# A hybrid decoder step on one core: where the decode attention gets its first operands, who splits its last values, and how the dense phase begins

## The chip, the cores and the metric

The kernel runs on one core of a Trainium2 chip. A time is the device time of one execution in microseconds (us). Three runs of the kernel before gave 1883.61, 1886.72 and 1889.7 us, so the median is 1886.72 us. The profile is one further execution of 1886.89 us.

## The reference, cut to what matters

One layer serves a prompt of 512 tokens and a sample group of 8 sequences with 8 new tokens each (64 rows). All arithmetic is float32.

```python
xn = rmsnorm(x, norm1_g);  proj = xn @ w_in          # q, k, v of 4 head sets, forget gates, 2 branch gates
q, k = rmsnorm per head (and rope in the 3 dilated sets)
# sample group, per sequence b: one paged set (FoX) and three windows
k_past = cache_fox_k[0][page_table]                   # 32 pages of 128 rows, 8 heads x 64
s = q @ k_past^T * scale + cnew + suffix(logf);  p = softmax(s with the 8 new keys);  o = p @ v_past + p_new @ v_new
# the same over window rows of cache_win1..3_kv, the three merged by their log-sum-exp
# prompt group: causal FoX attention and banded dilated attention
mixed = sigmoid(gate_a) * (o_fox @ w_branch_a) + sigmoid(gate_b) * (o_dil @ w_branch_b)
h = x + mixed @ w_out;  u = relu(rmsnorm(h) @ w_up);  y = h + (u * u) @ w_down
```

The outputs are y of both groups, the new k and v rows, the forget values and the shifted window caches.

## The kernel before, in words

Four functions run one after the other, with a barrier of all engines between them: `project_tokens` (0 to 488 us of the profile), `attend_sample` (488 to 1133), `attend_prompt` (1133 to 1341) and `finish` (1341 to the end). To keep float32 accuracy in the fast matmul form, each operand is split into a high part (a rounded copy, `*_hi`) and a low part (the difference, `*_lo`), and two or three products are summed.

`attend_sample` walks through 8 sequences (batches) of 24 groups each: 16 FoX groups of two pages, then 8 window groups of one or two tiles of 128 rows. A tile of K or V is 256 KB. Each engine has its own instruction stream, written out by `straight` (line 801): at step n an engine does each of its stages for group n minus the stage's delay. The stages of group i are:

- SP, step i: loads K of group i (`load_keys`) once group i - 6 is turned (a ring of 6 slots), with a load of the bias row for each even FoX group; step i + 20: loads V of group i (`load_values`), also in a ring of 6, freed when the low part of V of group i - 6 is made.
- PE, step i: turns K (transposes into `ktp`, line 1253); step i + 2: scores (line 1269); step i + 21: turns the probabilities; step i + 22: sums the values into `o_ps` (line 1285).
- ACT, step i: `kt_hi` (line 1082); step i + 20: exponentials and `vv_hi` (lines 1069 and 1090).
- DVE, step i + 1: `kt_lo` (line 1108); step i + 3: bias and maximum; step i + 21: the splits of the probabilities; in the last batch also `vv_lo` of two groups in three (line 1166).
- POOL, step i + 20: `vv_lo` (line 1024).

The `vv` buffers are a ring of 3, so `vv_hi` of group i waits for the sum of group i - 3.

Before its first K load, SP issues the page table and eight loads of the new queries and keys (lines 922 to 925), which lie as 64 columns inside the scratch tensors `qt_s` and `kt_s`. ACT and DVE split all of them first (lines 1052 and 1103) and POOL lays all queries out (line 998). At SP's step 2 come five small loads (lines 961 and 962): forget values, a triangle, two masks, and the new values `vs_raw`. A small matmul at PE's step 1 (line 1257) sums the new forget values in a bank of `s_ps`, and the first scores wait for its result. The new values are split by ACT at step 6 (line 1075) and POOL at step 8 (line 1007), both into buffers of the `vv` ring; SP stores them to scratch at step 14 in six stores (line 968). `qn_raw`, `kn_raw` and `vs_raw` lie in slots 0 to 3 of the V ring, which is why V loads come later.

`finish` begins with one weight slab (two halves: branch a, branch b) split by ACT (line 1862) and DVE (line 1929), then the attention output `o_all` split in two pieces of four tiles (lines 1867 and 1933); PE starts when the slab and the first piece are there (line 2016).

Of the kernel before, what the change touches and what calls it, by code (L numbers as in the profile page):

```python
# [13 lines left out]
P = 128  # L14
D_MODEL = 1024
SEQ = 512
# [42 lines left out]
def project_tokens(nc, a, sem, ident):  # L59

    with ExitStack() as ctx:
# [116 lines left out]
        def _(sp):  # L178
# [31 lines left out]
            sp.dma_start(cum[:], a["c_cum"]).then_inc(cum_in, 16)  # L210

# [26 lines left out]
            for s in range(SETS):  # L238
                g = s - 1
                for c in range(3):  # L240
# [532 lines left out]

def late_values(b, i):

    return isinstance(b, int) and b == DEC_BATCH - 1 and i >= PER_BATCH - EXP_BEHIND and i % 3 != 0
# [43 lines left out]
def attend_sample(nc, a, sem, ident, o_t, qk_raw, pair_in):  # L820

    with ExitStack() as ctx:
# [7 lines left out]
        pages = sb("pages", [1, DEC_BATCH * N_PAGES], I32)  # L830
# [45 lines left out]
        pages_in, in_small, queries_in, sample_v_in = sem("p2_pages_in"), sem("p2_small_in"), sem("p2_queries_in"), sem("p2_sample_v_in")  # L876
# [15 lines left out]
        held, v_lo_late = sem("held"), sem("v_lo_late")  # L892
# [9 lines left out]
        def values_split(eng, b, i):  # L902

            late = sum(late_values(b, n) for n in range(i + 1))
            if late_values(b, i):
                eng.wait_ge(v_lo_late, late)
            else:
                done(eng, v_lo, group_index(b, i) - late)
# [12 lines left out]
        def _(sp):  # L921
            sp.dma_start(pages[:], a["page_table"].rearrange("b n -> (b n)").unsqueeze(0)).then_inc(pages_in, 16)
            for s in range(SETS):
                sp.dma_start(qn_raw[:, s], a["qt_s"][s, :, :, SEQ:N_TOK].rearrange("q p n -> p q n")).then_inc(queries_in, 16)
                sp.dma_start(kn_raw[:, s], a["kt_s"][s, :, :, SEQ:N_TOK].rearrange("q p n -> p q n")).then_inc(queries_in, 16)
# [23 lines left out]
            def load_keys(b, i):  # L949
                done(sp, k_turned, group_index(b, i) - RAW_RING)  # L950
                hold(sp)
                load("K", a["cache_fox_k"], k_raw, k_in, b, i)
                if group_kind(i) == FOX and i % 2 == 0:
# [5 lines left out]
                if isinstance(b, int) and b == 0 and i == 2:  # L959
# [3 lines left out]
                if isinstance(b, int) and b == 0 and i == 14:  # L963
# [20 lines left out]
        def _(gp):  # L984
# [33 lines left out]
            def values_lo(b, i):  # L1018
                slot, tiles = i % VV_RING, group_tiles(i)
                if isinstance(b, int) and b == 0 and i == 0:  # L1020
                    gp.wait_ge(vs_stored, 96)
                if not late_values(b, i):
                    done(gp, v_hi, group_index(b, i))
                    gp.tensor_tensor(vv_lo[:, slot, 0:tiles, :], v_raw[:, i % RAW_RING, 0:tiles, :], vv_hi[:, slot, 0:tiles, :].bitcast(F32),  # L1024
                                     ALU.subtract).then_inc(v_lo, 1)
                if i == 7:
# [3 lines left out]
                    for part, x in enumerate((vn_hi, vn_lo)):  # L1030
# [16 lines left out]
        def _(act):  # L1047
            for s in (k_hi, v_hi, p_done):
                act.sem_inc(s, PER_BATCH)
            act.wait_ge(queries_in, 16 * 2 * SETS)  # L1050
            for dst, src in ((qn_hi, qn_raw), (kn_hi, kn_raw)):
                act.activation(dst[:], src, ACT.Copy).then_inc(parts_hi, 1)

            act.wait_ge(parts_lo, 2)
# [17 lines left out]
            def keys_hi(b, i):  # L1072
                if isinstance(b, int) and b == 0 and i == 6:
# [10 lines left out]
            def values_hi(b, i):  # L1084
# [1127 lines left out]
```

## Time and profile before

| | before |
|---|---|
| median of three runs | 1886.72 us (1883.61 to 1889.7) |
| profiled execution | 1886.89 us |
| its span, first to last instruction | 1885.1 us |
| PE / weight loads busy | 1739.2 / 1543.9 us (92% / 82%) |
| DVE, ACT, POOL busy | 1094.9, 956.1, 871.2 us |
| granted TensorE clock, mean | 0.97 |
| q1 (all loads and stores of SP) | 422.63 MB |

The execution is 1.8 us longer than its span; that part lies outside the program's instructions. The page divides the span into 40 slices of 47.1 us. In those from 500 to 1080 us PE and the DMA engines are both at nine tenths or more; in the dense phase after 1341 us only PE is.

### The profile page before, as it was taken

The numbers are of one execution on the slowest core, as the hardware profiler recorded it, in microseconds if no ns is written. First come the engines' busy times: TensorE is split into PE (matmuls) and PEld (weight loads), VectorE is DVE, ScalarE is ACT, GpSimd is POOL, SyncE is SP. The second block draws the span as 40 slices with busy tenths as digits, with TensorE's granted clock in tenths as the row PEclk, the third lists the DMA queues.
The fourth block names the chain that finished last, engine by engine and source line by source line (L and its number), as shares of the span: only waits on it lengthen the run. The fifth ranks groups of instructions, "written<-read, shape, count | busy, mean of one in ns | idle before, by whom it ended". The sixth has DMA issues, their size and how long they took to land. (4 is left out here: it accounts for less than half of the span.)

```text
span 1885.1 us, 32487 instructions
## 1 busy us (share of the span) xinstructions
PE 1739.2 (92%) x10749; PEld 1543.9 (82%) x10749; DVE 1094.9 (58%) x2474; ACT 956.1 (51%) x1644; POOL 871.2 (46%) x508
## 2 busy tenths in 40 slices
PE   7999999999599999999999976888799899999998
PEld 5787787899588889888888855777797889999897
DVE  6746546421287887888878877677443432424151
ACT  5434343332267777777777766778423322223130
POOL 2514333300147867778778746665232233333331
PEclk9999999999799999999999997899899999999999
DMA  6354363633699999999999979654445366656653
GB/s 225 92 174 132 104 193 103 201 120 106 183 338 339 324 334 326 335 326 322 341 329 322 315 221 273 180 175 137 144 135 218 145 257 267 245 223 267 244 225 116
DMA packets 226029, 426.74 MB, mean 226 GB/s; under 512 B 24457, under 2 KB 85770, under 8 KB 224466
## 3 DMA queue, kind: packets, MB, share of 16 engines
q1 hardware_dynamic: 222706, 422.63, 67.2%
q0 software_dynamic: 3168, 2.11, 0.5%
q8 instruction: 89, 1.46, 0.3%
q14 instruction: 66, 0.54, 0.1%
HBM read 392.36 MB, written 119.59 MB: 272 GB/s over the span
## 5 line engine op out<-in xcount | busy, mean ns | idle before, releaser
L1024 POOL TENSOR_TENSOR vv_lo<-v_raw,vv_hi 128x1024 fp32r<-128x1024 f32 x178 | 400.0, 2253 | 168.6 <-ACT vv_hi L1090 162.8
L1847 POOL TENSOR_TENSOR w_lo<-w_raw,w_hi 128x2048 fp32r<-128x2048 f32 x39 | 180.7, 4633 | 338.1 <-ACT w_hi L1862 338.1
L1082 ACT ACTIVATE kt_hi<-ktp 128x1024 fp32r<-128x1024 f32 (+1 forms) x192 | 186.2, 970 | 112.0 <-PE ktp L1253 109.0
L1108 DVE TENSOR_TENSOR kt_lo<-ktp,kt_hi 128x1024 fp32r<-128x1024 f32 (+1 forms) x192 | 220.8, 1150 | 8.6 <-ACT kt_hi L1082 6.7
L1253 PE MATMUL ktp<-ident,k_raw 128*128 128x128 f32 x1440 | 193.6, 277 | 21.0 <-DMA k_raw<-in_cache_fox_k 20.6
L1253 PEld LDWEIGHTS ktp<-ident,k_raw 128*128 128x128 f32 x1440 | 167.0, 142 | 51.2 <-DMA k_raw<-in_cache_fox_k 29.8
L1269 PE MATMUL s_ps<-kt_hi,q_st 128*128 128x256 f32 (+3 forms) x768 | 206.2, 301 | 0.8 <-DVE mx_parts L1148 0.8
L663 PE MATMUL acc<-w_hi,xn_hi 128*128 128x512 f32 x480 | 194.2, 405 | 2.4 <-POOL w_lo L302 2.4
L1090 ACT ACTIVATE vv_hi<-v_raw 128x1024 fp32r<-128x1024 f32 (+1 forms) x192 | 191.5, 997 | 6.9 <-PE o_ps L1285 5.9
L1269 PE MATMUL s_ps<-kt_lo,q_st 128*128 128x256 f32 (+3 forms) x768 | 191.1, 282 | 0.0
L663 PE MATMUL acc<-w_lo,xn_hi 128*128 128x512 f32 x480 | 189.8, 395 | 0.0
L1862 ACT ACTIVATE w_hi<-w_raw 128x2048 fp32r<-128x2048 f32 x40 | 76.6, 1915 | 201.2 <-PE acc L2041 156.4
L2041 PE MATMUL acc<-w_hi,right_hi 128*128 128x512 f32 x400 | 156.4, 391 | 0.0
L2041 PE MATMUL acc<-w_lo,right_hi 128*128 128x512 f32 x400 | 156.0, 390 | 0.0
L1285 PE MATMUL o_ps<-vv_hi,pt 128*128 128x512 f32 x360 | 148.3, 412 | 6.4 <-POOL vv_lo L1024 4.5
L663 PE MATMUL acc<-w_hi,xn_lo 128*128 128x512 f32 x384 | 152.6, 397 | 0.0
L1269 PEld LDWEIGHTS s_ps<-kt_hi,q_st 128*128 128x128 f32 x768 | 147.0, 191 | 3.7 <-issue 3.2
L1269 PEld LDWEIGHTS s_ps<-kt_lo,q_st 128*128 128x128 f32 x768 | 147.2, 192 | 0.0
L314 POOL TENSOR_TENSOR y_cos<-y_unit,rope_cg 128x512 f32<-128x512 f32 x40 | 51.7, 1293 | 203.7 <-DVE y_unit L564 195.2
L1285 PE MATMUL o_ps<-vv_lo,pt 128*128 128x512 f32 x360 | 143.6, 399 | 0.0
L1993 DVE TENSOR_TENSOR second<-first 128x576 f32<-128x576 f32 x32 | 87.3, 2728 | 93.8 <-ACT first L1912 93.8
L441 DVE TENSOR_TENSOR w_lo<-w_raw,w_hi 128x2048 fp32r<-128x2048 f32 x31 | 74.9, 2418 | 104.1 <-ACT w_hi L335 103.9
(243 smaller groups left out, 4195.0 us busy)
## 6 DMA issues: line engine op xcount, KB each, us to landing
k_raw<-in_cache_fox_k SPq DMA_DIRECT2D x256, 256.0 KB, 6.8
v_raw<-in_cache_fox_v SPq DMA_DIRECT2D x256, 256.0 KB, 6.2
out_win_kv_sample<-in_cache_win_kv SPq DMA_DIRECT2D x32, 2040.0 KB, 9.5
w_raw<-in_w_in SPq DMA_DIRECT2D x32, 1024.0 KB, 5.8
k_raw<-in_cache_win_kv SPq DMA_DIRECT2D x40, 512.0 KB, 10.5
v_raw<-in_cache_win_kv SPq DMA_DIRECT2D x40, 512.0 KB, 11.9
w_raw<-in_w_up SPq DMA_DIRECT2D x16, 1024.0 KB, 5.3
w_raw<-in_w_down SPq DMA_DIRECT2D x16, 1024.0 KB, 5.1
```

Of the source, the lines that this page charges most:

```text
L663: last = pe.matmul(acc[:, t, :], x[:, kk, t * P:t * P + P], w[:, k, :], start=(kk == 0 and i == 0), stop=(kk == KT - 1 and i == len(lots) ...
L1024: gp.tensor_tensor(vv_lo[:, slot, 0:tiles, :], v_raw[:, i % RAW_RING, 0:tiles, :], vv_hi[:, slot, 0:tiles, :].bitcast(F32), ALU.subtract). ...
L1082: act.activation(kt_hi[:, slot, :, 0:n], ktp[:, i % 2, :, 0:n], ACT.Copy).then_inc(k_hi, 1)
L1090: act.activation(vv_hi[:, slot, 0:tiles, :], v_raw[:, i % RAW_RING, 0:tiles, :], ACT.Copy).then_inc(v_hi, 1)
L1108: ve.tensor_tensor(kt_lo[:, slot, :, 0:n], ktp[:, i % 2, :, 0:n], kt_hi[:, slot, :, 0:n].bitcast(F32), ALU.subtract).then_inc(k_lo, 1)
L1253: last = pe.transpose(ktp[:, i % 2, q, n * P:(n + 1) * P], k_raw[:, i % RAW_RING, n, q * P:(q + 1) * P], ident[:])
L1269: last = pe.matmul(s_ps[:, i % S_RING, 0:wide], w, x, start=(n == 0), stop=(n == len(lots) - 1))
L1285: last = pe.matmul(o_ps[:], w, x, start=(group_first(i) and n == 0), stop=(group_last(i) and n == len(lots) - 1))
L1847: gp.tensor_tensor(w_lo[:, slot, :], w_raw[:, slot, :], w_hi[:, slot, :].bitcast(F32), ALU.subtract).then_inc(slab_lo_done, 1)
L1862: act.activation(w_hi[:, slot, :], w_raw[:, slot, :], ACT.Copy).then_inc(slab_hi_done, 1)
L1993: ve.tensor_tensor(second[:, f % 2, :], first[:, f % 2, :], first[:, f % 2, :], ALU.mult).then_inc(u_squared, 1)
L2041: last = pe.matmul(acc[:, (5 * c + t) % 8, :], x[:, kk, t * P:t * P + P], w[:, k, :], start=(kk == 0 and i == 0), stop=(kk == KT - 1 and i ...
```

## The change

Six edits, of which the first four concern the first batch of `attend_sample`.

1. The page table is loaded in `project_tokens`, among its constants. The new queries and keys get scratch tensors of their own, `qn_s` and `kn_s`, written with 64 columns per set in place of a padded tile; `qt_s` and `kt_s` shrink to the 512 prompt columns.
2. SP begins the decode phase with K of group 0, then one load of all queries; one load of all keys comes after K of group 8. The five small loads move from step 2 to step 7, and the six stores of the split new values from step 14 to step 17.
3. ACT, DVE and POOL split and lay out the FoX queries alone at first (set 0 of 4). The other queries follow at steps 3 to 5, the new keys at steps 11 to 13.
4. The small matmul moves from PE's step 1 to step 13 and to the bank `pt_ps`. DVE's addition of the mask follows at its step 14, POOL's copy of the result at step 14, and POOL's split of the new values at step 15.
5. In the last batch, DVE makes `vv_lo` of three groups in four instead of two in three (from group 4 on), and POOL makes `vv_hi` of one group in four.
6. `finish` splits the first slab and `o_all` piece by piece: half a slab, four tiles of `o_all`, the other half, four tiles; PE waits for each half and each tile.

```diff
@@ attend_sample, sync
-            sp.dma_start(pages[:], a["page_table"].rearrange("b n -> (b n)").unsqueeze(0)).then_inc(pages_in, 16)
-            for s in range(SETS):
-                sp.dma_start(qn_raw[:, s], a["qt_s"][s, :, :, SEQ:N_TOK].rearrange("q p n -> p q n")).then_inc(queries_in, 16)
-                sp.dma_start(kn_raw[:, s], a["kt_s"][s, :, :, SEQ:N_TOK].rearrange("q p n -> p q n")).then_inc(queries_in, 16)
             sp.wait_ge(pages_in, 16)
...
                 load("K", a["cache_fox_k"], k_raw, k_in, b, i)
+                if b == 0 and i == 0:
+                    sp.dma_start(qn_raw, a["qn_s"]).then_inc(qn_in, 16)
+                if b == 0 and i == 8:
+                    sp.dma_start(kn_raw, a["kn_s"]).then_inc(kn_in, 16)
...
-                if isinstance(b, int) and b == 0 and i == 14:
+                if b == 0 and i == 17:
                     sp.wait_ge(vs_lo_done, 1)
@@ attend_sample, gpsimd: per_batch
-                    if i == 8:
+                    if i == 10:
+                        gp.wait_ge(in_small, 64)
+                        gp.tensor_copy(lfn_wide[:]..., lfn_raw[:]...).then_inc(wide_laid, 1)
+                    if i == 5:
+                        gp.wait_ge(parts_lo, 2)
+                        lay_queries(WIN, 0)
+                    if i == 14:
+                        gp.wait_ge(new_biased, 1)
+                        gp.tensor_copy(bias[:, PAST_LEN:], bias_new[:, 0, :]).then_inc(bias_tail, 1)
+                    if i == 15:
                         gp.wait_ge(vs_hi_done, 1)
                         gp.tensor_tensor(vs_lo, vs_raw, vs_hi.bitcast(F32), ALU.subtract).then_inc(vs_lo_done, 1)
@@ values_lo
+                if late_high(b, i):
+                    arrived(gp, v_in, b, i)
+                    done(gp, v_summed, group_index(b, i) - VV_RING)
+                    gp.tensor_copy(vv_hi[:, slot, 0:tiles, :], v_raw[:, i % RAW_RING, 0:tiles, :]).then_inc(v_hi_late, 1)
@@ attend_sample, scalar: keys_hi
+                if b == 0 and i == 3:
+                    act.activation(qn_hi[:, 1:], qn_raw[:, 1:], ACT.Copy).then_inc(parts_hi, 1)
+                if b == 0 and i == 11:
+                    act.wait_ge(kn_in, 16)
+                    act.activation(kn_hi[:], kn_raw, ACT.Copy).then_inc(parts_hi, 1)
@@ attend_sample, vector: keys_lo
+                if b == 0 and i == 12:
+                    ve.wait_ge(parts_hi, 3)
+                    ve.tensor_tensor(kn_lo[:], kn_raw, kn_hi[:].bitcast(F32), ALU.subtract).then_inc(parts_lo, 1)
+                if b == 0 and i == 13:
                     ve.wait_ge(new_summed, 1)
@@ finish, scalar (vector and tensor follow the same pieces)
-            slab_part(0, 1, 0)
             for kind in (FOX, WIN):
-                part = slice(kind * PAIRS, (kind + 1) * PAIRS)
-                act.activation(left_hi[:, part, 0:N_TOK], o_raw[:, part, :], ACT.Copy).then_inc(o_hi_done, 1)
+                cols = slice(kind * SLAB // 2, (kind + 1) * SLAB // 2)
+                act.activation(w_hi[:, 0, cols], w_raw[:, 0, cols], ACT.Copy).then_inc(first_hi_done, 1)
+                for part in range(kind * PAIRS, (kind + 1) * PAIRS):
+                    act.activation(left_hi[:, part, 0:N_TOK], o_raw[:, part, :], ACT.Copy).then_inc(o_hi_done, 1)
```

SP before, from K of groups 13 and 14 to the first window groups; `vn_s` is the scratch of the new values, a K row of 128x512 is one page:

```order
L943 DMA k_raw<-in_cache_fox_k 128x512
L958 DMA bias<-sfx_s 64x1x512
L968 DMA vn_s<-vv_hi 64x512 x2
L968 DMA vn_s<-vv_hi 64x2x512
L968 DMA vn_s<-vv_lo 64x512 x2
L968 DMA vn_s<-vv_lo 64x2x512
L943 ISA
L943 DMA k_raw<-in_cache_fox_k 128x512
L943 ISA
L943 DMA k_raw<-in_cache_fox_k 128x512
L947 DMA k_raw<-in_cache_win_kv 128x512
L947 DMA k_raw<-in_cache_win_kv 128x2x512 x4
```

And now, from K of group 15:

```order
L961 DMA k_raw<-in_cache_fox_k 128x512
L965 DMA k_raw<-in_cache_win_kv 128x512
L965 DMA k_raw<-in_cache_win_kv 128x2x512
L990 DMA vn_s<-vv_hi 64x512 x2
L990 DMA vn_s<-vv_hi 64x2x512
L990 DMA vn_s<-vv_lo 64x512 x2
L990 DMA vn_s<-vv_lo 64x2x512
L965 DMA k_raw<-in_cache_win_kv 128x2x512 x3
L951 TENSOR_LOAD pages
L961 ISA
L961 DMA v_raw<-in_cache_fox_v 128x512
```

The stores stood behind K of group 14 and stand behind K of group 17; K of group 18 and the first V load are now the next loads behind them.

POOL in the last batch before (from group 4 on; `vn_hi` and `vn_lo` are loads of new values):

```order
L1024 TENSOR_TENSOR vv_lo<-v_raw,vv_hi 128x1024 x5
L1032 DMA vn_hi<-vn_s 8x512
L1033 DMA vn_hi<-vn_s 24x1x512
L1032 DMA vn_lo<-vn_s 8x512
L1033 DMA vn_lo<-vn_s 24x1x512
L1024 TENSOR_TENSOR vv_lo<-v_raw,vv_hi 128x1024 x5
```

And now:

```order
L1060 TENSOR_TENSOR vv_lo<-v_raw,vv_hi 128x1024 x5
L1057 CAST vv_hi<-v_raw 128x1024
L1068 DMA vn_hi<-vn_s 8x512
L1069 DMA vn_hi<-vn_s 24x1x512
L1068 DMA vn_lo<-vn_s 8x512
L1069 DMA vn_lo<-vn_s 24x1x512
L1060 TENSOR_TENSOR vv_lo<-v_raw,vv_hi 128x1024
L1057 CAST vv_hi<-v_raw 128x1024
L1060 TENSOR_TENSOR vv_lo<-v_raw,vv_hi 128x1024
L1057 CAST vv_hi<-v_raw 128x1024
L1060 TENSOR_TENSOR vv_lo<-v_raw,vv_hi 128x512
```

POOL's five differences behind the loads of new values became a mix of differences and five copies in all.

DVE at the start of `finish`, before:

```order
L1927 MEMSET eps_col 128x1
L1929 TENSOR_TENSOR w_lo<-w_raw,w_hi 128x2048
L1933 TENSOR_TENSOR left_lo<-o_all,left_hi 128x4x576 x2
L1941 TENSOR_TENSOR first<-acc,gates 128x576
```

And now:

```order
L1971 MEMSET eps_col 128x1
L1975 TENSOR_TENSOR w_lo<-w_raw,w_hi 128x1024
L1978 TENSOR_TENSOR left_lo<-o_all,left_hi 128x576 x4
L1975 TENSOR_TENSOR w_lo<-w_raw,w_hi 128x1024
L1978 TENSOR_TENSOR left_lo<-o_all,left_hi 128x576 x4
```

Three differences became ten smaller ones in another order; ACT's stream is cut in the same way.

## Rows read from the trace of the kernel before

**Rows 1.** The page: the chain that ended last, by line.

```profile
PE acc L2041 13%; PE acc L2071 11%; PE acc L2016 3%; DVE qk_raw L1982 0%; ACT qk_raw L1894 0%; DVE left_lo L1965 0%; DVE h L1954 0%; DVE left_lo L1933 0%; DVE w_lo L1929 0%; ACT w_hi L1862 0%; PE acc L2027 0%; ACT std L1896 0%; DVE h L1958 0%; DVE h L1956 0%; DVE rstd L1977 0%
```

**Rows 2.** Windows: length, busy time of engines, clock, DMA share, GB/s.

```profile
504.00:508.00 4.00, 1.10 (x5) 0.98 (x6) 1.44 (x2) 0.38 (x1) 0.41 (x2) 0.50 1.00 197
512.00:516.00 4.00, 4.00 (x36) 3.92 (x35) 3.59 (x8) 2.41 (x3) 0.00 (x0) 1.00 1.05 343
540.00:544.00 4.00, 4.00 (x34) 3.67 (x33) 3.59 (x9) 1.16 (x3) 0.00 (x0) 1.00 1.05 388
580.00:600.00 20.00, 18.85 (x136) 16.24 (x134) 14.64 (x40) 14.36 (x24) 15.75 (x8) 1.00 1.05 333
```

**Rows 3.** Timeline of SP's issues, 488 to 537 us: start, length, what.

```profile
488.70 0.25 SPq L922 DMA_DIRECT2D pages<-in_page_table  x1
...
494.68 0.90 SPq L943 DMA_DIRECT2D k_raw<-in_cache_fox_k  x2
...
524.33 1.80 SPq L968 DMA_DIRECT2D vn_s<-vv_hi  x3
...
528.61 2.50 SPq L943 DMA_DIRECT2D k_raw<-in_cache_fox_k  x2
531.22 4.47 SPq L947 DMA_DIRECT2D k_raw<-in_cache_win_kv  x5
```

**Rows 4.** Timeline of PE: groups 0, 2 and 18 turned.

```profile
497.99 1.97 PE L1253 MATMUL ktp<-ident,k_raw 128*128 128x128 f32 x8 [13.74 <-DMA k_raw<-in_cache_fox_k]
...
507.31 1.97 PE L1253 MATMUL ktp<-ident,k_raw 128*128 128x128 f32 x8
...
542.85 1.04 PE L1253 MATMUL ktp<-ident,k_raw 128*128 128x128 f32 x8
```

**Rows 5.** Timeline of DVE, 510 to 536 us: `kt_lo` of groups 2 and 13.

```profile
510.37 1.23 DVE L1108 TENSOR_TENSOR kt_lo<-ktp,kt_hi 128x1024 fp32r<-128x1024 f32 x1 [2.74 <-ACT kt_hi L1082]
...
535.01 1.21 DVE L1108 TENSOR_TENSOR kt_lo<-ktp,kt_hi 128x1024 fp32r<-128x1024 f32 x1
```

**Rows 6.** Timeline of POOL, 500 to 519 us.

```profile
500.43 0.26 POOL L998 CAST q_st<-qn_hi 64x96 fp32r<-64x96 f32 x1
...
518.17 4.59 POOL L1007 TENSOR_TENSOR vv_lo<-v_raw,vv_hi 64x2048 fp32r<-64x2048 f32 x1 [10.29 <-ACT vv_hi L1075]
```

**Rows 7.** DMA view, 520 to 536 us: issues, KB each, median us to landing.

```profile
k_raw<-in_cache_win_kv SPq DMA_DIRECT2D x4, 512.0 KB, 7.1
```

**Rows 8.** Waits of 575 to 603 us: total, times, longest.

```profile
PEld ktp L1253 <- DMA k_raw<-in_cache_fox_k: 3.1, 5, 0.8
```

**Rows 9.** Timelines of ACT, DVE and POOL, last batch.

```profile
1099.23 1.06 ACT L1090 ACTIVATE vv_hi<-v_raw 128x1024 fp32r<-128x1024 f32 x1 [0.49 <-PE o_ps L1285]
...
1104.22 1.06 ACT L1090 ACTIVATE vv_hi<-v_raw 128x1024 fp32r<-128x1024 f32 x1
...
1102.24 1.65 DVE L1166 TENSOR_TENSOR vv_lo<-v_raw,vv_hi 128x1024 fp32r<-128x1024 f32 x1
...
1104.33 1.22 DVE L1166 TENSOR_TENSOR vv_lo<-v_raw,vv_hi 128x1024 fp32r<-128x1024 f32 x1
...
1100.38 2.43 POOL L1024 TENSOR_TENSOR vv_lo<-v_raw,vv_hi 128x1024 fp32r<-128x1024 f32 x1 [0.40 <-ACT vv_hi L1090]
```

**Rows 10.** Window of the last batch, columns as in rows 2.

```profile
1105.00:1110.00 5.00, 4.17 (x20) 2.58 (x19) 4.28 (x9) 4.67 (x10) 2.44 (x1) 1.00 0.91 329
```

**Rows 11.** Timelines of ACT, DVE and PE, start of the dense phase.

```profile
1341.45 1.91 ACT L1862 ACTIVATE w_hi<-w_raw 128x2048 fp32r<-128x2048 f32 x1 [0.89 <-PEq L2191]
1343.26 4.12 ACT L1867 ACTIVATE left_hi<-o_all 128x2304 fp32r<-128x2304 f32 x2
...
1343.39 2.29 DVE L1929 TENSOR_TENSOR w_lo<-w_raw,w_hi 128x2048 fp32r<-128x2048 f32 x1 [1.83 <-ACT w_hi L1862]
1345.60 5.02 DVE L1933 TENSOR_TENSOR left_lo<-o_all,left_hi 128x2304 fp32r<-128x2304 f32 x2
...
1348.29 0.82 PE L2016 MATMUL acc<-left_hi,w_hi 128*128 128x288 f32 x2 [8.37 <-DVE left_lo L1933]
```

More of the change, by code:

```diff
@@ L56, in products, with project_tokens @@
     return 3 if t < Q_TILES else 2
-def project_tokens(nc, a, sem, ident):
+def project_tokens(nc, a, sem, ident, pages, pages_in):
     with ExitStack() as ctx:
@@ L210, in _ @@
             sp.dma_start(cum[:], a["c_cum"]).then_inc(cum_in, 16)
+            sp.dma_start(pages[:], a["page_table"].rearrange("b n -> (b n)").unsqueeze(0)).then_inc(pages_in, 16)
             def store_forget():
@@ L771, in new_rows, with late, late_high @@
     return (DEC_SEQ if group_kind(i) == FOX else WIN_NEW) if group_last(i) else 0
+def late(b, i):
+    return b == DEC_BATCH - 1 and i >= PER_BATCH - EXP_BEHIND
 def late_values(b, i):
-    return isinstance(b, int) and b == DEC_BATCH - 1 and i >= PER_BATCH - EXP_BEHIND and i % 3 != 0
+    return late(b, i) and i % 4 != 0
+def late_high(b, i):
+    return late(b, i) and i % 4 == 2
 def stream(eng, runs, length, *stages):
@@ L902, in values_split, with high_split @@
         def values_split(eng, b, i):
-            late = sum(late_values(b, n) for n in range(i + 1))
+            count = sum(late_values(b, n) for n in range(i + 1))
             if late_values(b, i):
-                eng.wait_ge(v_lo_late, late)
+                eng.wait_ge(v_lo_late, count)
             else:
-                done(eng, v_lo, group_index(b, i) - late)
+                done(eng, v_lo, group_index(b, i) - count)
+        def high_split(eng, b, i):
+            count = sum(late_high(b, n) for n in range(i + 1))
+            if late_high(b, i):
+                eng.wait_ge(v_hi_late, count)
+            else:
+                done(eng, v_hi, group_index(b, i) - count)
         def pieces(i):
@@ L1049, in _ @@
                 act.sem_inc(s, PER_BATCH)
[L1050 to L1054, printed above, removed]
+            act.wait_ge(qn_in, 16)
+            act.activation(qn_hi[:, 0], qn_raw[:, 0], ACT.Copy).then_inc(parts_hi, 1)
             def out_low(b, i):
@@ L1227, in turn_probs @@
                     pe.wait_ge(zeroed, 2)
+                    pe.wait_ge(new_biased, 1)
                 hold(pe)
@@ L1254, in turn_keys @@
                 last.then_inc(k_turned, 1)
-                if isinstance(b, int) and b == 0 and i == 1:
+                if b == 0 and i == 13:
                     pe.wait_ge(wide_laid, 1)
-                    pe.matmul(s_ps[0:HT, 1, 0:N_SAMPLE], lfn_wide[:], new_tri[:], start=True, stop=True).then_inc(new_summed, 1)
+                    pe.matmul(pt_ps[0:HT, 0:N_SAMPLE], lfn_wide[:], new_tri[:], start=True, stop=True).then_inc(new_summed, 1)
             def score(b, i):
```

103 lines of the change are left out of this document (58 added, 45 removed).

## The prediction

> **What bounds the kernel now.** I read the page first, then the chain of waits, the windows through the three places that the change touches, each engine's timeline there, and the waits.
>
> The chain of waits shows that from the first matmul of the dense phase PE runs to the end almost without a break; behind its two big lines stand only short pieces on ACT and DVE [rows 1, 11]. So whatever makes that first matmul earlier comes off the end, and so does every microsecond by which an earlier phase ends earlier, since the phases are parted by barriers.
>
> The decode phase has three stretches. At its start PE does nothing useful: SP issues the page table at 488.70, its first K at 494.68, PE turns it at 497.99, but group 2 only at 507.31, behind the small matmul [rows 3, 4]. Then come groups without V work: `kt_lo` of group 2 starts at 510.37, that of group 13 at 535.01, 24.6 us for 11 groups, mostly steps of 2.19, so 24.1 without two disturbances [rows 5]. From step 20 on K and V are loaded together. There DMA stands at 1.05 of its share, which is as high as it goes, at 333 GB/s, with PE busy 18.85 of 20 us [rows 2]. A step with two FoX groups needs 1.05 MB plus half a bias row of 0.13 MB, 1.11 MB or 3.3 us at 333 GB/s, against PE's usual step of about 3. So the ring of loaded groups drains there, and the waits show where it is empty: PE's weight loads wait five times, 3.1 us together, for FoX K between 575 and 603 [rows 8]. This is the row on which most of my forecast rests: in the first two batches the DMA schedule decides, and the lead that it had at group 18 is used up by about 600 us.
>
> **The change, part by part.** All times are those of the profiled execution (1886.89 us, 1885.1 of it span, 0.17 above the median of the runs).
>
> *Early start (gain).* SP's first K no longer waits for the page table and eight loads. It needs about 1 us for reading the pages, so it goes out at 489.7 in place of 494.68, 5 us earlier. K of group 0 takes the 3.3 us of before (494.68 to 497.99) and is turned at 493. Group 1 comes when two K groups, the queries and one bias row (0.52 + 0.52 + 0.52 + 0.13 = 1.7 MB) have passed at 343 GB/s [rows 2], 5 us after the flow begins at about 490.8, so 495.8; two turns of 1.7 at half clock, group 2 starting at 497.5. In the trace `kt_lo` of group 2 starts 3.06 after its turn (507.31, 510.37), so now at 500.6: 9.8 us earlier. The queries (ACT, DVE, four POOL copies of at most 0.26 [rows 6]) are laid out by about 496, before the first scores. The scratch stores of the projection phase keep their number; they lie beside PE's matmuls, 0.
>
> *Work moved into the first steps (loss).* These steps are as long as DVE's work in them. DVE now has the rest of the queries (three quarters of a 1.23 us difference, 0.9) and the keys (1.2) there; ACT's two extra splits fit its gaps but for some 0.4. Sum 2.5, between 1.5 and 3.
>
> *The small loads behind group 7 and the keys behind group 8.* Up to K of group 7 SP asks for 5.24 MB, 15.3 us at 343 GB/s, done at 506.1. The small loads are 0.97 MB; they ran at 197 GB/s with the DMA share at 1.00 [rows 2], which is 4.9 us, or 2.8 at the full rate. The keys add 0.52 MB, 1.5 us. K of group 9 then lands at 516, where DVE's pace wants it at 513.8: 2.2 late; the bounds are 0 (small loads at the full rate) and 4. Sum up to `kt_lo` of group 13: 500.6 + 24.1 + 2.5 + 2.2 = 529.4, against 535.01.
>
> *The stores behind group 17 (loss, and what is late next).* SP may issue K of group 17 as soon as group 11 is turned, some 7 us before that moment. Behind it stands the wait for the split of the new values, and that now hangs on a chain: `kt_lo` of group 13 at 529.4, 1.2 for it, 0.3 for the masked sum, 0.3 for POOL's copy and semaphores, 4.59 for POOL's difference [rows 6]: 535.8. Before, POOL had done it at 522.8, and SP came to the stores at 524.33 without a wait [rows 3]. The six stores take SP 4.28 (524.33 to 528.61): K of group 18 goes out at 540.1. Everything is queued behind it on SP: all later K and the first V. With the 3.3 us of group 0 it lands at 543.4, while PE by its own pace would want it at about 536.6. PE turns it 0.55 later than before (542.85) [rows 4]: of the 9.8 us nothing is left, and the ring is empty. Before, K of group 18 went out between 532 and 533.6, inside the row of five loads [rows 3], and landed by 539 to 540.7 with the 7.1 us of such loads [rows 7]: a lead of 2.1 to 4.3 us. By the argument on rows 8 the lead that is missing turns into PE waits before 600 us. So the decode phase comes out 0.55 + 3.2 = 3.8 later, between 2.7 and 4.9 if the rest holds. If nothing were late in the DMA queue (2.2 gone), 1.6; if 4 were late, 5.6.
>
> *The last batch.* Groups there take 4.99 us per three (1099.23 to 1104.22): `vv_hi` 1.06, POOL's 2.43, the sum, and again `vv_hi` in the same slot [rows 9]. With POOL at one low part in four that cycle goes. The next limits stand close: DVE had 4.28 of 5 us busy for three groups with two differences [rows 10]; for four groups with three I get 4 x 0.53 + 3 x 1.22 + 0.44 = 6.2, 1.56 per group against 1.66; DMA was at 0.91 there. POOL's copy of 128x1024 has no row: it lies between 0.26 (96 elements) and the 2.43 of the two-input form; I take 1.2, half of it, since it reads one input. Over about nine groups the gain is 0.9; bounds: gain 2.5 (ACT, freed of five splits, and the window groups profit too), loss 1.5. I take 0.8.
>
> DVE's difference took 1.65 beside POOL's (1102.24) and 1.22 alone (1104.33): POOL's ended at 1102.81, and the DVE instruction lasted about 1.1 more [rows 9]. The Trainium skill, "SBUF — State Buffer", section "SBUF: two separate sides", says that VectorE and GpSimd share a port pair as an exclusive lock, for a VectorE instruction with two SBUF inputs against a GpSimd one that reads SBUF; by that rule, the trace agrees. It would make POOL's new copies hold DVE up as well, and the gain of this part would be 0 in place of 0.8.
>
> *The dense phase begins with pieces (gain).* Before: slab high part 1.91, low part 2.29, first piece of `o_all`, PE at 1348.29 [rows 11]. Now ACT's half slab takes 1.0 (1341.45 to 1342.45); DVE's half 1.2 to 1343.7; the first tile (5.02 for eight, so 0.65) to 1344.4; PE at 1344.55, 3.7 earlier. Behind it nothing is late: at the half clock that PE has there a tile's matmuls take 1.44 (three pairs of 0.48), DVE makes one in 0.65; the second half slab is ready by 1347.6 and the fifth tile by 1348.3, when PE is in its third. POOL's next slab comes about a microsecond later and is wanted 12 us after. Bounds: gain 2.5 to 4.
>
> Sum: + 3.8 - 0.8 - 3.7 = - 0.7, so 1886.2; I say 1886. Of small changes nothing under 0.3% (5.7 us) can be told from none.
>
> **The rivals.**
>
> *The lead isn't needed.* PE's pace, not the DMA schedule, sets the first batches. For it: PE is busy 18.85 of 20 us, and all later waits on K are short. Against: rows 8. Then only PE's turn of group 18 counts, with nothing late in the DMA queue: 541.2 against 542.85, and the phase ends 1.6 earlier: - 1.6 - 0.8 - 3.7 = - 6.1, 1880.8. If K of group 18 even comes in time, because the chain before POOL's difference is shorter than I count, all of 9.8 - 2.5 = 7.3 stays: - 11.8, 1875.
>
> *The drained ring costs more (slower).* PE stands idle some 5 us at group 18 and its clock may fall; it was at 0.50 while PE stood idle around 504 [rows 2]. The K and V loads then start from an empty ring, and every FoX step takes 3.3 in place of 3: if the ring stays empty through the second and third batch as well, each of about 20 steps costs another 0.3, 6 us on top of 5.6: 5.6 + 6 - 0.8 - 3.7 = + 7.1, 1894. It decides from the point where group 18 lands over 2 us later than before. Against it: window groups need less and refill the ring.
>
> *The dense phase gains nothing*, because PE, fed tile by tile, waits for a semaphore at each: rows 11 have DVE at less than half of PE's pace, so I give it almost nothing; it would be 1890.
>
> **How the numbers follow.** Forecast (1881.2 to 1892): 0.48. Lead not needed or stall small (1874 to 1881): 0.39, part of it still within 0.3%. Drained ring: 0.09. Dense phase: 0.04. Faster by over 0.3% (below 1881.1) 0.38, within 0.3% 0.53, slower 0.09. The range goes from 1876 to 1891; that of the likeliest case alone is 1882 to 1891.
>
> **What would show it.** Right: the first K goes out about 5 us earlier, `kt_lo` of group 2 about 10 us earlier; SP issues the `vn_s` stores about 11 us later than before, and K of group 18 right behind; PE waits 4 to 7 us for a window K there; PE's waits for K between 575 and 603 grow over 3.1. The first dense matmul starts 3.1 after ACT's first split there, in place of 6.8. Wrong: no long wait for a window K, or the end of decode earlier than before by over 3 us.

## The result, and the profile after

The changed kernel takes 1897.63 us (median of 7 runs, 1892.31 to 1900.7) against 1886.6 (7 runs, 1883.61 to 1889.7): 1.005 times the time of before, 95% interval 1.0034 to 1.0066, so some 10 us slower (11 by the medians). The forecast was 1886, its range ended at 1891. The profiled execution took 1898.93 us, 1897.1 of it span, at a mean clock of 0.967; before it was 1886.89, 1885.1 and 0.970.

The timeline of DVE through the first batch of the changed kernel shows where (`kt_lo` of groups 2, 7, 8, 9, 13, 17 and 18; it answers to [rows 5]):

```profile
506.24 1.23 DVE L1143 TENSOR_TENSOR kt_lo<-ktp,kt_hi 128x1024 fp32r<-128x1024 f32 x1 [0.28 <-ACT kt_hi L1116]
...
519.53 1.23 DVE L1143 TENSOR_TENSOR kt_lo<-ktp,kt_hi 128x1024 fp32r<-128x1024 f32 x1 [1.21 <-ACT kt_hi L1116]
527.03 1.23 DVE L1143 TENSOR_TENSOR kt_lo<-ktp,kt_hi 128x1024 fp32r<-128x1024 f32 x1 [5.22 <-ACT kt_hi L1116]
531.31 1.23 DVE L1143 TENSOR_TENSOR kt_lo<-ktp,kt_hi 128x1024 fp32r<-128x1024 f32 x1 [2.01 <-ACT kt_hi L1116]
...
541.94 1.21 DVE L1143 TENSOR_TENSOR kt_lo<-ktp,kt_hi 128x1024 fp32r<-128x1024 f32 x1
...
550.30 1.21 DVE L1143 TENSOR_TENSOR kt_lo<-ktp,kt_hi 128x1024 fp32r<-128x1024 f32 x1
560.60 1.22 DVE L1143 TENSOR_TENSOR kt_lo<-ktp,kt_hi 128x1024 fp32r<-128x1024 f32 x1 [7.63 <-ACT kt_hi L1116]
```

Group 2 comes 4.1 us earlier than before, group 13 comes 6.9 later, and from group 17 to 18 it takes 10.3 us where it took 2.6. There are two jumps, groups 7 to 9 (11.8 us for two steps of 2.19) and 17 to 18. In this run the projection phase also ended 2.8 us later; over the sixteen kernels profiled here the decode phase starts anywhere from 488.6 to 492.2, with kernels of the same code up to it 3 us apart, so the table below counts from there (DVE's first memset of the decode phase).

SP's issues, at the small loads, the keys of the new tokens, the stores and K of group 18 (answers to [rows 3]):

```profile
506.16 0.50 SPq L983 DMA_DIRECT2D lfn_raw<-lf_s  x1
...
508.61 0.64 SPq L984 DMA_DIRECT2D v_raw<-v_s  x1
...
511.34 0.43 SPq L974 DMA_DIRECT2D v_raw<-kn_s  x1
...
533.05 2.23 SPq L965 DMA_DIRECT2D k_raw<-in_cache_win_kv  x2
548.10 1.80 SPq L990 DMA_DIRECT2D vn_s<-vv_hi  x3
...
552.04 2.38 SPq L965 DMA_DIRECT2D k_raw<-in_cache_win_kv  x3
```

The waits of 484 to 600 us (total, times, longest), first SP's own, then PE's (answer to [rows 8]):

```profile
SPq L990 <- POOL vv_lo L1039: 12.8, 1, 12.8
```

```profile
PEld ktp L1295 <- DMA k_raw<-in_cache_fox_k: 21.6, 6, 10.3
...
PEld ktp L1295 <- DMA k_raw<-in_cache_win_kv: 7.4, 1, 7.4
```

Windows of the two stretches (columns as in [rows 2]):

```profile
508.00:512.00 4.00, 4.00 (x33) 3.60 (x31) 3.69 (x8) 2.29 (x3) 0.00 (x0) 1.00 1.02 217
512.00:516.00 4.00, 2.33 (x17) 1.87 (x16) 3.56 (x7) 1.03 (x1) 1.06 (x4) 1.00 1.12 150
516.00:520.00 4.00, 2.66 (x16) 2.39 (x16) 2.59 (x7) 1.02 (x1) 0.23 (x1) 0.81 1.02 201
540.00:544.00 4.00, 2.88 (x24) 2.54 (x24) 3.59 (x8) 1.02 (x1) 0.65 (x2) 1.00 0.15 55
544.00:548.00 4.00, 3.45 (x26) 2.79 (x25) 3.76 (x8) 2.09 (x6) 4.00 (x1) 1.00 0.00 0
```

In the first, the DMA engines are full (share over 1.00) and move 150 to 217 GB/s for 12 us, where a K stretch moves 343 [rows 2]. The DMA view of 508 to 520 us, and of the 6 us before the small loads (500 to 506), shows that the low rate holds for everything in the queue, K included:

```profile
DMA packets 1250, 2.27 MB, mean 189 GB/s; under 512 B 345, under 2 KB 345, under 8 KB 1249
k_raw<-in_cache_fox_k SPq DMA_DIRECT2D x8, 256.0 KB, 12.3
```

```profile
DMA packets 1178, 2.14 MB, mean 357 GB/s; under 512 B 131, under 2 KB 131, under 8 KB 1178
k_raw<-in_cache_fox_k SPq DMA_DIRECT2D x8, 256.0 KB, 6.2
```

Half of a K group lands 12.3 us after its issue in place of 6.2, and nearly the same bytes take 12 us in place of 6. In the second they are empty: SP stands at the stores, waiting for POOL's difference (543.50, 4.57 us), and everything that PE will want is queued behind it. The clock fell back to 0.50 after both.

POOL in the last batch, beside DVE and alone (answers to [rows 9]), and the start of the dense phase on ACT and PE (answers to [rows 11]):

```profile
1110.41 2.00 POOL L1057 CAST vv_hi<-v_raw 128x1024 fp32r<-128x1024 f32 x1
...
1117.82 2.03 POOL L1057 CAST vv_hi<-v_raw 128x1024 fp32r<-128x1024 f32 x1
...
1124.96 2.04 POOL L1057 CAST vv_hi<-v_raw 128x1024 fp32r<-128x1024 f32 x1
...
1132.81 1.04 POOL L1057 CAST vv_hi<-v_raw 128x1024 fp32r<-128x1024 f32 x1 [1.76 <-PE o_ps L1325]
```

```profile
1356.64 1.06 ACT L1907 ACTIVATE w_hi<-w_raw 128x1024 fp32r<-128x1024 f32 x1 [0.90 <-PEq L2245]
...
1359.77 0.82 PE L2063 MATMUL acc<-left_hi,w_hi 128*128 128x288 f32 x2 [4.66 <-DVE left_lo L1978]
```

From ACT's first split to the first dense matmul it is 3.13 us, where it was 6.84.

The table gives stretches of every kernel that ran, in us: from the start of decode to `kt_lo` of group 8, 17 and 18; from there to group 36; from `kt_lo` of the last group to the prompt phase; and the median with the ratio to before (95%). The kernel before was run beside each of them on the same chip, and the ratio is taken against those runs, so that kernels from different chips are compared by their ratios. Medians and ratios leave out one single run of kernel A, which took 5975.54 us.

| kernel | to 8 | to 17 | to 18 | 18 to 36 | end | median | ratio |
|---|---|---|---|---|---|---|---|
| before | 34.7 | 53.9 | 56.4 | 52.9 | 45.8 | 1886.6 | |
| changed | 34.9 | 58.1 | 68.4 | 55.0 | 47.0 | 1897.6 | 1.0034 to 1.0066 |
| A values split early | 35.9 | 57.7 | 60.3 | 54.0 | 46.3 | 1887.3 | 0.9992 to 1.0021 |
| B small loads at 2 | 37.0 | 57.5 | 67.8 | 56.3 | 47.5 | 1895.8 | 1.0038 to 1.0080 |
| A and B | 35.1 | 55.5 | 58.1 | 50.8 | 46.5 | 1883.0 | 0.9973 to 1.0001 |
| C old last batch | 34.5 | 56.7 | 67.1 | 57.0 | 43.6 | 1896.5 | 1.0039 to 1.0075 |
| A, B, C | 36.9 | 57.4 | 60.0 | 52.8 | 43.4 | 1884.6 | 0.9976 to 1.0002 |
| before + dense pieces | 36.5 | 56.0 | 58.6 | 52.7 | 43.1 | 1881.1 | 0.9960 to 0.9989 |
| the same + new last batch | 36.6 | 55.8 | 58.3 | 53.5 | 47.0 | 1882.9 | 0.9962 to 0.9996 |
| A + mask at 12 | 32.6 | 58.5 | 61.1 | 56.4 | 47.0 | 1888.3 | 0.9998 to 1.0021 |
| A, C, spread loads | 31.3 | 57.4 | 60.0 | 52.6 | 46.7 | 1886.6 | 0.9981 to 1.0013 |
| values as four loads | 30.4 | 58.4 | 60.9 | 52.9 | 46.8 | 1888.1 | 1.0000 to 1.0031 |
| other source | 30.0 | 58.3 | 60.8 | 52.8 | 46.4 | 1889.5 | 1.0004 to 1.0040 |
| 128 partitions | 28.4 | 57.4 | 60.0 | 51.4 | 46.8 | 1885.4 | 0.9983 to 1.0011 |
| dense pieces + four loads | 36.0 | 55.2 | 57.7 | 53.0 | 45.9 | 1880.7 | 0.9954 to 0.9984 |
| first batch rearranged | 40.7 | 59.9 | 62.4 | 51.3 | 45.2 | 1884.9 | 0.9966 to 0.9996 |

### The profile page after: what moved, and what is told of

It reads as the page before. It is cut to its first block and busy times, and to the rows that moved or that the text cites. A ratio compares the mean times of both kernels' runs of the same rounds, so it can differ in the third digit from the quotient of the medians.

```text
span 1897.1 us, 32513 instructions
## 1 busy us (share of the span) xinstructions
PE 1745.2 (92%) x10749; PEld 1551.4 (82%) x10749; DVE 1097.7 (58%) x2483; ACT 952.9 (50%) x1647; POOL 877.4 (46%) x512
## 5 line engine op out<-in xcount | busy, mean ns | idle before, releaser
L1295 PE MATMUL ktp<-ident,k_raw 128*128 128x128 f32 x1440 | 197.6, 281 | 33.0 <-DMA k_raw<-in_cache_fox_k 25.1
L1126 ACT ACTIVATE vv_hi<-v_raw 128x1024 fp32r<-128x1024 f32 (+1 forms) x187 | 186.5, 997 | 9.6 <-PE o_ps L1325 8.5
```

The lines of the kernel that those rows point to most:

```text
L1126: act.activation(vv_hi[:, slot, 0:tiles, :], v_raw[:, i % RAW_RING, 0:tiles, :], ACT.Copy).then_inc(v_hi, 1)
L1295: last = pe.transpose(ktp[:, i % 2, q, n * P:(n + 1) * P], k_raw[:, i % RAW_RING, n, q * P:(q + 1) * P], ident[:])
```

## The experiments

**A, the new values split early.** Only what SP waits for is moved, not the order of its queue. One wait is added: SP waits for the low parts of the new keys before its first V load, which overwrites the place of the unsplit keys.

```
+                if b == 0 and i == 0:         # SP: before the first V load
+                    sp.wait_ge(parts_lo, 3)
...
-                if b == 0 and i == 12:        # ACT: vs_hi
+                if b == 0 and i == 9:
...
-                    if i == 15:               # POOL: vs_lo
+                    if i == 11:
```

> Changed kernel, but the new values are split earlier (ACT's high part at group 9 in place of 12, POOL's difference at group 11 in place of 15), so that SP finds it done when it comes to the stores behind group 17; the order of SP's queue is untouched. Theory S (two separate stalls in the first batch: a backlog of the DMA queue behind group 7, and SP's wait of 12.8 us at the stores, which makes K of group 18 late): SP's wait at the stores goes, the step of kt_lo from group 17 to 18 falls from 10.3 us to about 3, and the run is 7 to 8 us faster than the changed kernel, about 1890. Rival L (the loss is a lead of loaded groups that is used up later, wherever SP stood): the stall only moves to groups 20 to 34, and the run stays at 1896 to 1898.

1887.3 us (10 runs). SP's wait is gone, the stores and K of group 18 go out one behind the other, and the step from 17 to 18 is 2.58 again:

```profile
532.31 1.80 SPq L990 DMA_DIRECT2D vn_s<-vv_hi  x3
534.16 3.04 SPq L990 DMA_DIRECT2D vn_s<-vv_lo  x3
537.31 2.69 SPq L965 DMA_DIRECT2D k_raw<-in_cache_win_kv  x3
```

```profile
546.93 1.21 DVE L1145 TENSOR_TENSOR kt_lo<-ktp,kt_hi 128x1024 fp32r<-128x1024 f32 x1
...
549.51 1.21 DVE L1145 TENSOR_TENSOR kt_lo<-ktp,kt_hi 128x1024 fp32r<-128x1024 f32 x1
```

The stall moved nowhere: the wait was worth 10 us by the medians, more than the 7 to 8 that S had; 7.7 of them stand where it was, and between groups 18 and 36 these two traces differ by another 1.1 (the three kernels with the stall take 55.0 to 57.0 us from group 18 to 36, those without 50.8 to 54.0 but for one of 56.4). Theory S holds for this stall.

**B, the small loads behind group 2 again** (`i == 7` to `i == 2` in `load_keys`).

> Changed kernel, but with the small loads behind group 2, where they were before, and not behind group 7; the keys of the new tokens stay behind group 8 and the stores behind 17. Theory S: the backlog of 508 to 520 us shrinks to the keys' own 1.5 us, kt_lo of groups 8 to 17 comes 6 to 9 us earlier, and since the chain before the stores begins at group 13, all of it stays: 1889 to 1891. Rival K (the keys behind group 8, not the small loads, make the backlog): kt_lo of group 13 gains under 2 us, 1896 to 1898. Rival C (the start is bound by DVE's added splits): the same as K, but without PE waiting for FoX K between 505 and 535 us.

1895.82 us (7 runs): 1.8 less, where S wanted 6.6 to 8.6. To group 17 it is 57.5 against 58.1. The jump only moved: from group 2 to 3 it now takes 7.7 us. So the backlog goes with the small loads wherever they stand, and S was wrong in that half: it had the backlog shrink to the keys' own 1.5 us. The number is as rival K had it, the mechanism isn't: the keys still stand behind group 8, and from group 7 to 9 it takes 4.4 us, the pace without a wait.

**A and B together.**

> Both edits together (small loads behind group 2, and the new values split at groups 9 and 11). Theory S: the two add up, 1881 to 1884, which is 3 to 5 us faster than the kernel before. Rival L: 1888 or more, because what the start gains is lost by group 34.

1883.0 us (11 runs), the number of S; L is out. That the number fits is in part luck, since A gave more than S had and B less. Against the kernel before, the interval of the ratio (0.9973 to 1.0001) doesn't exclude "the same". But group 17 comes 55.5 us after the start, no earlier than in the kernel before (53.9) or in the three other kernels with its start (55.2 to 56.0): the early start is gone by then.

**C, the last batch as before** (`late_values` at `i % 3 != 0`, no `late_high`).

> Changed kernel with the last batch as before: POOL makes every third low part and no high part. My reading of the traces (the changed kernel runs 1.79 us per group there, the one before 1.66, and the offset of the decode phase grows from 17.6 to 18.5 over it): 1 to 2 us faster than the changed kernel, 1896. Rival as I forecast (the new last batch gains 0.8): 1898.5.

1896.54 us (5 runs), 1.1 less, inside the intervals of both.

**The dense pieces alone**, on the kernel before.

> The kernel before with nothing but the new beginning of the dense phase (half slabs, and the tiles of the attention output one by one). As forecast, which the trace of the changed kernel shows (first dense matmul 3.1 us after ACT's first split in place of 6.8): 3.7 us faster than before, 1883. Rival: the gain is given back in the dense phase, because PE then waits at the second half slab or for POOL's next slab: 1885 to 1887.

1881.06 us (8 runs), 0.9975 of before (0.996 to 0.9989). In its trace:

```profile
1340.11 1.06 ACT L1867 ACTIVATE w_hi<-w_raw 128x1024 fp32r<-128x1024 f32 x1 [0.89 <-PEq L2198]
```

```profile
1343.24 0.82 PE L2023 MATMUL acc<-left_hi,w_hi 128*128 128x288 f32 x2 [4.65 <-DVE left_lo L1938]
```

The gain of 3.7 us (6.84 to 3.13 us of lead) is there and stays: from the first dense matmul to the end it is 535.9 us, where it was 536.8; the interval of the ratio, 2 to 7.5 us, holds it.

**A, B and C.**

> Small loads behind group 2, new values split at groups 9 and 11, and the last batch as before; early start and dense pieces stay. If the last batch as before is 1 to 4 us better in this surrounding too (it was 1.1 by the medians, more by the trace), 1879 to 1882. If it only looked so, 1883 as without that edit.

1884.61 us (12 runs), no better than without C. Against the dense pieces alone, run beside it on the same chip, what it has more is the early start and the work moved with it: 3.5 us slower by the medians, with intervals that overlap.

**The mask behind group 12** (with A).

> The version with the new values split early (1887.5), with one of the small loads, the window mask of 0.42 MB, moved from behind group 7 to behind group 12. Theory V (the slow stretch of the DMA queue, 150 to 210 GB/s for 12 us, is made by each small load in proportion to its bytes): about 40% of the stretch goes from group 8 and returns behind group 12 beside ring slack; PE's wait at group 8 falls from 6 us to about 3, the run is 2 to 3 us faster, 1885. Rival W (the new values' load of 64 partitions alone makes it, or the keys'): group 8 gains only the 1.2 us that 0.42 MB take at 343 GB/s, 1886.5 to 1887.

1888.3 us (11 runs), no gain. From group 7 to 9 it takes 11.2 us against 12.4 without the edit: 1.2 less, which is the mask's bytes at the full rate, the number of rival W. But the traces side with V. In A's the queue is slow for 11 us; here for 7, and again for 2 behind group 12, where the mask now is (window of A, then two of this kernel):

```profile
507.00:518.00 11.00, 6.35 (x48) 5.40 (x47) 9.21 (x18) 3.16 (x4) 1.29 (x5) 1.00 1.06 173
```

```profile
509.00:516.00 7.00, 4.60 (x37) 3.97 (x35) 6.35 (x14) 2.55 (x3) 1.05 (x4) 1.00 1.06 181
524.00:526.00 2.00, 1.10 (x6) 0.81 (x4) 1.48 (x2) 2.00 (x2) 0.00 (x0) 0.74 1.01 117
```

PE's wait for K of group 8 falls from 6.0 to 2.6 us, as V had it; in exchange PE waits 2.7 us for K of group 9 and, behind the mask's load, 2.8 for that of group 13. The mask too lies in 64 partitions. So the slow stretch was moved in part, and nothing was gained.

**Spread loads**: A, C, small loads behind group 5, mask behind 12.

> As the version with last batch as before and new values split early, but the small loads and the new values' load behind group 5 (where SP would wait for the ring anyway), the mask behind group 12, the keys behind group 8. Theory: spread, they lie in the queue's slack between 1.7 us per group that it needs and 2.19 that the engines take, so kt_lo of group 17 comes 2 to 3 us earlier than with all small loads behind group 2: 1877 to 1880. Rival: the start is one queue's volume, whatever the order: as with the small loads behind group 2.

1886.64 us (12 runs). Group 8 comes at 31.3, earliest so far, group 17 at 57.4, not earlier than with all small loads behind group 2 (55.5 and 57.4). The number is the rival's.

**The rows of the new values as four loads**, with A and the mask behind 12.

```
-  sp.dma_start(vs_raw, a["v_s"][:, SEQ:N_TOK].rearrange("s p n -> p s n")).then_inc(sample_v_in, 16)
+  for s in range(SETS):
+      sp.dma_start(vs_raw[:, s], a["v_s"][s, SEQ:N_TOK]).then_inc(sample_v_in, 16)
```

> The version with the mask behind group 12 (1888.3), with the load of the new values' rows (0.5 MB into 64 partitions, four rows of 2 KB into each) issued as four loads, one per set, so that neighbouring rows go to different partitions. Theory P (rows that follow each other into the same partition are slow): the stretch of 150 to 250 GB/s behind group 7 goes, and kt_lo from group 7 to 9 takes 5 to 6 us in place of 11.2. Rival H (64 partitions alone, or the source, is slow): still 10 to 12 us. By the median 3 to 5 us faster under P, the same under H.

1888.1 us (12 runs). Groups 7 to 9 take 8.6 us, between P and H, but the queue is still at 195 GB/s with its share at 1.04 from 508 to 516: P falls.

**The same load from another source.**

> The version with the mask behind group 12, with the new values' rows read from the K cache (same shape, same rows of 2 KB, same destination), so its values are not those of the reference; the work is the same. Theory M (reading the scratch tensor, whose four sets lie one fixed distance apart, is slow): the slow stretch goes, 5 to 6 us from group 7 to 9. Theories P and H (the destination is what is slow): 10 to 12 us as before.

1889.47 us (10 runs), 7.9 us from group 7 to 9, neither as M nor as H had it. The window of 508 to 516 us:

```profile
508.00:516.00 8.00, 6.27 (x50) 5.51 (x48) 7.17 (x15) 3.12 (x4) 1.29 (x5) 1.00 1.06 204
```

The source isn't it: 204 GB/s. The 11.2 us of the kernel that it is compared with also hold a clock that fell to 0.71.

**Twice the bytes into twice the partitions.**

```
+  wide_raw = early[:, 2 * SETS * PAIRS * N_SAMPLE:][:, 0:SETS * D_HEADS] ...   # all 128 partitions
+  src = a["cache_fox_k"][0, 0:SETS].rearrange("s p h d -> p s (h d)")
+  sp.dma_start(wide_raw, src).then_inc(sample_v_in, 16)
```

> The version with the mask behind group 12, with the new values' rows replaced by a load of 1 MB from the K cache into the same columns of all 128 partitions (twice the bytes, rows of 2 KB as before), so its values are not those of the reference. Theory H (64 partitions are what makes the slow stretch, 0.5 MB in 4 to 5 us): 1 MB at 343 GB/s takes 3.1 us, so kt_lo from group 7 to 9 is no longer than 11.2 us and rather 7 to 8, and the packets of the stretch are fast. Rival B (something else makes the stretch, a backlog of the queue behind group 7): twice the bytes make it longer, 12 us or more.

1885.37 us (10 runs). The same window:

```profile
508.00:516.00 8.00, 7.04 (x52) 5.99 (x53) 7.35 (x14) 3.48 (x4) 1.28 (x5) 1.00 1.05 374
```

374 GB/s with 1 MB in place of 204 with 0.5 MB, same rows, same source, same place: the loads into 64 partitions are what takes the queue's time. Groups 7 to 9 take 7.1 us although 0.5 MB more has to pass.

Yet group 17 comes at 57.4, as in kernels whose group 8 is 3 to 8 us later. The mask behind group 12, still in 64 partitions, makes a stretch of its own here too, and PE waits for K of group 13:

```profile
519.00:522.00 3.00, 2.60 (x12) 2.60 (x13) 0.62 (x3) 0.60 (x1) 3.00 (x1) 0.54 1.01 134
```

```profile
533.10 1.97 PE L1304 MATMUL ktp<-ident,k_raw 128*128 128x128 f32 x8 [3.19 <-DMA k_raw<-in_cache_fox_k]
```

From group 12 to 14, four of the five kernels with the mask there take 6.6 to 10.3 us, and all the others 4.4 to 5.7. This kernel takes 10.3 there and A 5.7, so the second 64-partition load takes back 4.6 of the 7.5 us by which group 8 comes earlier than in A. No kernel ran with both out of the way.

**Four loads on the best kernel.**

> The kernel before with the new beginning of the dense phase (1881.1), and the new values' rows loaded as four loads at their old place behind group 2. Theory P: the wait before group 3 or 2 there (6.0 to 6.8 us between kt_lo of groups 1 and 2) shrinks by 2 to 3 us, 1878 to 1879. Rival H: 1881.

1880.7 us (12 runs, ratio 0.9954 to 0.9984), the same as with one load (1881.1). P is out here too. With the dense pieces alone this is the fastest kernel of the study; both beat the kernel before and the changed one.

**The new last batch on the dense pieces.**

> The kernel before with the new beginning of the dense phase (1881.1) and the new last batch (POOL one low part in four and one high part in four). By the traces so far the stretch from kt_lo of group 168 to the prompt phase takes 118.7 to 121.6 us in five kernels with the new last batch and 115.5 to 118.8 in five with the old one: 2 to 3 us slower, 1883.5. Rival, as I forecast: 0.8 faster, 1880.

1882.88 us (12 runs) against 1881.06: not decided by the medians. The traces lean one way: from `kt_lo` of the last group to the prompt phase this kernel takes 47.0 us against 43.1. Over all kernels it is 46.3 to 47.5 with the new last batch (nine) and 43.1 to 46.7 with the old one (seven), means 46.8 and 44.8; only one of the seven lies inside the range of the nine.

```profile
L1190 DVE TENSOR_TENSOR vv_lo<-v_raw,vv_hi 128x1024 fp32r<-128x1024 f32 x13 | 18.3, 1408 | 1.2 <-POOL vv_hi L1043 0.8 <-ACT vv_hi L1114 0.4
```

```profile
L1166 DVE TENSOR_TENSOR vv_lo<-v_raw,vv_hi 128x1024 fp32r<-128x1024 f32 x11 | 14.9, 1355 | 0.0
```

These are DVE's low parts of two tiles (128x1024) from 1090 to 1128 us, in this kernel and in the one with the old last batch: there are more of them, as the edit wants, each takes 53 ns longer, and they wait 0.8 us for POOL's high part.

**The first batch rearranged**: dense pieces, early start, keys right behind the queries, every added split where DVE waits for K.

> Early start and dense pieces of the changed kernel, the last batch as before, and the first batch arranged so that every added split lies where DVE and ACT wait for the DMA queue anyway: keys loaded right behind the queries, small loads behind group 2, the rest of the queries and the keys split at groups 2 and 3, the new tokens' bias at group 4, new values split at groups 6 and 8, stores behind group 14. Theory Q (the start is bound by the queue's volume until about group 8; what the changed kernel lost besides the stores is DVE work put behind that point): kt_lo of group 17, counted from the start of the phase, comes 1 to 2 us earlier than in the kernel before, and the run takes 1878 to 1880, 1 to 3 us less than with the dense pieces alone (1881). Rival: the early start is worth nothing, because the queue moves the same bytes: 1881 to 1883.

1884.94 us (12 runs, 0.9966 to 0.9996): faster than before, but by its median slower than the dense pieces alone (the intervals of the two ratios overlap). Group 8 comes 40.7 us after the start, the latest of all, and 17 at 59.9. Theory Q falls. The queue had three windows in a row like these:

```profile
500.00:504.00 4.00, 1.89 (x8) 1.57 (x8) 0.10 (x1) 0.00 (x0) 0.00 (x0) 0.50 1.13 199
504.00:508.00 4.00, 1.58 (x8) 1.50 (x8) 1.22 (x1) 1.02 (x1) 0.00 (x0) 0.50 1.03 160
508.00:512.00 4.00, 2.15 (x11) 1.88 (x9) 2.44 (x3) 2.70 (x3) 0.51 (x2) 0.75 1.04 202
```

## Why the prediction was wrong, step by step

- *Early start.* Forecast for group 2: 9.8 us earlier. Measured 4.1, or 6.9 counted from the start of the phase. The first K went out 0.5 us after DVE's first memset (492.67), as I had it. The way from there to group 2 was mis-sized: K of group 1 was turned 9.0 us behind SP's first K (501.67), where I had 6.1. I let the queue move 343 GB/s from the start; it moved 141 from 492 to 496 and 271 from 496 to 500.
- *Work moved into the first steps.* Forecast 2.5. What the steps outside the jumps show: 0.6 at group 5 and 1.3 at groups 13 and 14, so 1.9 and part of the 1.3 at group 7. Right.
- *The small loads and the keys.* This is the step that failed first: "K of group 9 then lands at 516, where DVE's pace wants it at 513.8: 2.2 late", with a bound of 4. Groups 7 to 9 took 11.8 us where 4.4 is their pace, 7.4 late, and more at groups 7 and 10. I had taken the right rate for the 64-partition loads, 197 GB/s, for their own bytes, 4.9 us. The queue was slow for 12 us, and PE turned K of group 9 only at 528.25. That 64 partitions make it slow is shown (204 against 374 GB/s). What I had wrong is whose bytes go slowly: in those 12 us 2.27 MB passed at 189 GB/s, the small loads' 0.97 MB and with them the keys, bias rows and K of the next groups. At my 197 GB/s these 2.27 MB would be 11.5 us (an estimate). It is longest where the keys stand right behind the small loads: counted in slices of 1 us below 230 GB/s, the stretch has 11 in the three kernels with the keys right behind all small loads, 10 in the rearranged one, 5 to 9 in those with the small loads behind group 2 and the keys elsewhere. Why a K load into 128 partitions slows down beside one into 64 is not shown. Sum: `kt_lo` of group 13 was forecast at 529.4 and came at 541.94.
- *The stores.* The mechanism was as forecast: chain over group 13 and POOL (4.57 us), SP waiting, DMA empty, PE waiting for a window K, 7.4 us where I expected 4 to 7. Its start was 12 us later than I thought, because the chain hangs on group 13. From group 17 to 18 it cost 7.7 us.
- *The lost lead.* Forecast 3.2 us as PE waits between 575 and 603. Group 18 came 14.8 us later than before, so the same groups now stand up to 618; the waits of 589 to 618 in the changed kernel are

```profile
PEld ktp L1295 <- DMA k_raw<-in_cache_fox_k: 3.7, 5, 1.9
```

against 3.1 [rows 8], 0.6 more; in B and C, which have the stall too, they are 5.2 and 6.6 (575 to 618), but in A, which has not, they are 4.2. From group 18 to 36 it takes 2.2 us more than before, and 3.4 and 4.1 in B and C. In the changed kernel 1.6 of the 2.2 fall on groups 18 to 20, right behind the stall, where the granted clock was 0.50 (556 to 560 us). So the cost has about the forecast size, but in this trace most of it is not the wait that I named.
- *The last batch.* Forecast a gain of 0.8; the traces have a loss of 2.0 in the mean over all kernels, 1.2 between before and changed. POOL's copy of 128x1024 takes 2.0 us beside DVE and 1.04 alone; I had taken 1.2. The row that spoke against it stood in the prediction, the DVE difference of 1.65 beside POOL and 1.22 alone [rows 9]; I named it and still took 0.8 into the sum. By the rule of the Trainium skill cited there, which the trace bears out (1.04 us alone, 2.0 beside DVE), the gain of this part would have been 0. The copies follow each other at 7.14 us for four groups (1117.82 to 1124.96), 1.79 per group where I had 1.56 and the kernel before 1.66; which wait makes the loss was not taken apart.
- *The dense phase.* Forecast 3.7, measured 3.71. Right.

Against the profiled run of before: projection + 2.8 (which differs from run to run), to group 17 + 4.3, to 18 + 7.7, to 36 + 2.2, to the last group + 0.7, its end + 1.2, prompt phase - 3.6, dense start - 3.7; with the rounding that is 11.5 of the 12.0 us; the rest lies behind the first dense matmul (537.3 us to the end against 536.8). The prompt phase takes 204.0 to 208.6 us over all kernels, with no part of it changed, so its - 3.6 is run to run too. My rival "the drained ring costs more" had the sign and 1894, at a chance of 0.09. Its condition held (group 18 landed more than 2 us late, and the clock fell to 0.50), but its 6 us in the second and third batch didn't come: `kt_lo` is 17.0 us behind at group 36 and 15.0 at group 76. The loss stood before group 20, so the rival is nearer by luck. What I should have asked is how late the chain *starts* if the queue is slow: both terms hang on the same row, and I added their middles.

## What to carry to other kernels

A wait in the queue that issues all loads costs everything behind it, so what it waits for must be done by the time that the queue can come there at its earliest; breaking that chain was worth 10 us here, moving instructions on two engines by a few groups. Starting a stream of loads earlier gave nothing here, because the queue was full soon after: the same bytes pass, and vector work that lay under the waits for data may end up behind them. Where small loads go into half of the partitions, count at half the rate not only their bytes but those of everything that is queued among them; moving one of them moves the slow stretch and doesn't remove it.

## What I had not expected of the hardware

- A load into partitions 0 to 63 keeps all DMA engines busy at half the rate: 204 GB/s against 374 at 128 partitions, with a share of 1.06 and 1.05. The Trainium skill, "SBUF — State Buffer", section "Door 1: The DMA port swizzle (why `[64,N]` ≈ `[32,N]`)", says that partitions 0 to 63 reach only 8 of 16 ports, and gives 196 and 328 GB/s at 1 MiB; the trace agrees with the first figure (204), and has more than the second (374). The row was there before the change: 197 GB/s at a share of 1.00 [rows 2].
- K loads into 128 partitions are as slow while such a load is in the queue: 12.3 us from issue to landing in place of 6.2, and 2.27 MB in 12 us where 2.14 MB took 6. Why, is open.
- A GpSimd copy with one input also takes twice its time beside VectorE's two-input differences (2.0 against 1.04 us); those of 128x1024 took 1408 ns in the mean with such copies among them, 1355 without.
- Phases with the same code differ by 2 to 4 us from run to run (start of decode 488.6 to 492.2, prompt phase 204.0 to 208.6), so a term of 2 us shows in a stretch of a trace before it shows in medians of ten runs.
